# A state space by blocks of four tokens, and forty modulation chunks moved from one mixer to two feed-forwards

## The reference, cut to what matters

```python
# the state space: 16 groups g of 16 channels h, 64 complex states p each, tokens s
ab = exp((lr + 1j * li) * dt)                      # one complex factor per state (ab_re, ab_im)
bu[s, g, p] = sum_h ug[s, g, h] * bb[g, p, h]      # complex
x[s] = ab * x[s - 1] + bu[s]                       # the scan over the tokens
y[s, g, h] = Re(sum_p c[g, h, p] * x[s, g, p]) + d_skip[g, h] * ug[s, g, h]
z = gelu(y);  y_c = z * sigmoid(z @ w_glu + b_glu)
```

```python
mod   = silu(c)    @ w_mod[l] + b_mod[l]    # 6 * 1024 columns: sh1, sc1, g1, sh2, sc2, g2
mod_c = silu(c_cx) @ w_mod[l] + b_mod[l]
```

## Time and profile before

| | us |
|---|---|
| median of 3 runs | 1832.56 |
| lowest, highest | 1821.2, 1836.75 |
| the profiled execution | 1824.21 |
| its span, first to last instruction | 1822.4 |

### The profile page before, as it was taken

The page is one execution under the profiler, slowest core; times in us unless marked ns, Lnnn a source line. Parts: engine busy times, 40 slices in busy tenths (PEclk is TensorE's granted clock), DMA queues, the critical chain, the costliest instruction groups (busy, mean ns, idle before and its releaser), DMA issues.

```text
span 1822.4 us, 28979 instructions
## 1 busy us (share of the span) xinstructions
PE 1780.3 (98%) x9846; PEld 1443.9 (79%) x9846; DVE 804.6 (44%) x1556; ACT 903.1 (50%) x1410; POOL 1378.4 (76%) x811
## 2 busy tenths in 40 slices
PE   9989999999999999999999999999999999999997
PEld 7768888766888887788888977788888987788886
DVE  5566773674454554443112555441114665441112
ACT  6455443645544544555444455564436445554443
POOL 7359997546988878578888884578887894678884
PEclk9999999999999999999999999999999999999999
DMA  7767785687878646346665552346654563346551
GB/s 272 192 215 255 257 263 198 213 278 272 287 264 259 227 139 191 109 140 192 202 194 175 171 185 93 126 153 206 196 187 149 172 208 105 112 149 193 189 188 70
DMA packets 259110, 348.28 MB, mean 191 GB/s; under 512 B 20936, under 2 KB 161608, under 8 KB 259016
## 3 DMA queue, kind: packets, MB, share of 16 engines
q1 hardware_dynamic: 255840, 340.44, 58.1%
q10 hardware_dynamic: 3176, 6.62, 1.2%
HBM read 343.24 MB, written 1.64 MB: 189 GB/s over the span
## 4 chain that ended last, share of the span: by engine, by line
PE 89%; DVE 5%; ACT 2%; issue 1%; DMA 1%; POOL 1%; SPq 0%; ACTq 0%; DVEq 0%; POOLq 0%
PE bank L2402 23%; PE bank L2404 23%; PE bank L2403 23%; PE bank L2541 2%; PE bank L3119 2%; PE bank L2472 1%; PE bank L2470 1%; PE bank L2471 1%; PE bank L3109 1%; PE bank L3158 1%; PE bank L2507 1%; PE bank L2774 1%; PE bank L2565 0%; ACT wh L859 0%; DVE X L1552 0%
## 5 line engine op out<-in xcount | busy, mean ns | idle before, releaser
L827 POOL TENSOR_TENSOR wl<-raw,wh 128x1024 fp32r<-128x1024 f32 x300 | 734.4, 2460 | 101.7 <-ACT wh L1024 78.0
L2402 PE MATMUL bank<-wh,xh 128*128 128x512 f32 (+1 forms) x1590 | 625.2, 393 | 9.6 <-POOL wl L787 2.8
L2404 PE MATMUL bank<-wl,xh 128*128 128x512 f32 (+1 forms) x1590 | 611.4, 385 | 0.0
L2403 PE MATMUL bank<-wh,xl 128*128 128x512 f32 (+1 forms) x1590 | 610.0, 384 | 0.0
L786 POOL TENSOR_TENSOR wl<-raw,wh 128x512 fp32r<-128x512 f32 (+1 forms) x232 | 310.7, 1339 | 282.9 <-ACT wh L859 282.8
L1024 ACT ACTIVATE wh<-raw 128x1024 fp32r<-128x1024 f32 x270 | 286.7, 1062 | 430.2 <-PE bank L2404 417.6
L859 ACT ACTIVATE wh<-raw 128x1024 fp32r<-128x1024 f32 (+2 forms) x268 | 275.4, 1049 | 167.4 <-PE bank L2404 89.5
L2402 PEld LDWEIGHTS bank<-wh,xh 128*128 128x128 f32 x1590 | 299.0, 188 | 73.9 <-issue 8.5
L2404 PEld LDWEIGHTS bank<-wl,xh 128*128 128x128 f32 x1590 | 298.7, 188 | 60.9
L2403 PEld LDWEIGHTS bank<-wh,xl 128*128 128x128 f32 x1590 | 299.4, 188 | 54.8
L787 POOL TENSOR_TENSOR wl<-raw,wh 128x512 fp32r<-128x512 f32 (+1 forms) x232 | 310.5, 1339 | 0.0
(11 more groups left out here) (399 smaller groups left out, 2041.3 us busy)
## 6 DMA issues: line engine op xcount, KB each, us to landing
raw<-in_w_ffn_in SPq DMA_DIRECT2D x264, 256.0 KB, 2.9
raw<-in_w_in SPq DMA_DIRECT2D x224, 256.0 KB, 2.9
raw<-in_w_ffn_out SPq DMA_DIRECT2D x132, 256.0 KB, 2.9
raw<-in_w_mod SPq DMA_DIRECT2D x120, 256.0 KB, 4.4
raw<-in_l_w_gate SPq DMA_DIRECT2D x88, 256.0 KB, 3.7
raw<-in_l_w_up SPq DMA_DIRECT2D x88, 256.0 KB, 4.4
raw<-in_l_w_down SPq DMA_DIRECT2D x88, 256.0 KB, 4.2
arena<-in_w_mod SPq DMA_DIRECT2D x36, 512.0 KB, 5.5
```

What stands on the lines that cost most here:

```text
L827: nc.gpsimd.tensor_tensor(wl[:, s, :], raw[:, s, :], words(wh)[:, s, :], ALU.subtract)\
L2402: mm(dst, x_hi, w_hi, start=first, stop=False, skip_group_check=True)
L2403: mm(dst, x_lo, w_hi, start=False, stop=False, skip_group_check=True)
L2404: return mm(dst, x_hi, w_lo, start=False, stop=last, skip_group_check=True)
```

## The change

**Modulation.** Of layer 1 only tiles 0 and 1 (8 chunks) stay on PE in the second mixer. The other ten tiles go the second way: ten blocks in `ffn_c0` and ten in `ffn_x0`, the feed-forwards of the two streams in layer 0 of the second block. These get DVE's 16 operations a step, the loads beside the ring, and `mod_add` and `mod_turn` at their ends.

**State space.** The tokens are taken in blocks of four. A group of 16 channels is laid out so that 4 tokens by 32 channels of a pair fill the 128 partitions, and 64 blocks are the columns: `block_rows` does this with 64 fp32 matmuls of 32 columns on strips. `drive(c)` now serves four pairs at once (8 matmuls of 64 columns with full weights), so that there are two rounds c = 0, 1 and not eight. The scan runs over blocks with the fourth power of the decay, four pairs in one scan row, all on DVE; POOL has no part in it. `state(c)` adds, for each of the 4 tokens of a block, what the state of the block before gives (8 matmuls of 63 columns) and what the block's own tokens give (4 matmuls of 64 columns with the matrix `near`, d_skip in it); these are on strips of 32 columns. `near` comes from `near_products` (32 matmuls of 128 columns on strips, twice) and `near_matrix` on DVE. The tables `bpow`, `cpow` and the powers of the factor are made in `discretise` and `state_tables`. The 1 MB load of `c_re` and `c_im` in the mixer and ACT's negation of `c_im` go; smaller tables are loaded with `b_re` and `b_im`. ACT's Gelu reads the bank itself, and DVE's skip operations go.

```diff
-PE_MOD_TILES = (3, 12)
-LATE_MOD = {"ffn0": (0, 3, 8), "ffn1": (0, 7, 10)}
+PE_MOD_TILES = (3, 2)
+LATE_MOD = {"ffn0": (0, 3, 8), "ffn1": (0, 7, 10), "ffn_c0": (1, 2, 10), "ffn_x0": (1, 7, 10)}
+MOD_TURN = {"ffn0": 1, "ffn1": 3, "ffn_c0": 4, "ffn_x0": 5}
...
-    plan.modulation("mod1_lat", 1, w_mod[1], 3)
-    each = {n: (1, w_mod[1]) for n in range(3)}
-    plan.gemm("uq", a["l1_w_uq"], [384] * 3, modulated=each)
-    plan.gemm("ukv", a["l1_w_ukv"], [512] * 3, modulated=each)
-    plan.modulation("mod1_rope", 1, w_mod[1], 3)
-    for u in range(2 * MH):
-        plan.modulation(f"mod1_mla{u}", 1, w_mod[1], 2)
-    plan.gemm("out1", a["l1_w_out"], [512] * 2, pair=0, k_groups=[range(2, KD), range(0, 2)], modulated={0: each[0]})
+    plan.gemm("uq", a["l1_w_uq"], [384] * 3)
+    plan.gemm("ukv", a["l1_w_ukv"], [512] * 3)
+    plan.gemm("out1", a["l1_w_out"], [512] * 2, pair=0, k_groups=[range(2, KD), range(0, 2)])
     plan.modulation("mod1_norm", 1, w_mod[1], 4)
...
-                if name == "out1":
-                    for j in range(POOL_STATES, SSM_J):
-                        spin(j)
-                        state(j)
...
-                reduced(th16, ki, kf)
-                n = spread(C_("count").unsqueeze(1), SSM_J, 16)
-                step(v.tensor_tensor(angle[:, :, 0:16], n, spread(th.unsqueeze(2), SSM_J, 16), ALU.mult))
-                step(v.tensor_tensor(angle[:, :, 16:], n, spread(th16.unsqueeze(2), SSM_J, 16), ALU.mult))
+                step(v.tensor_scalar(th4, th, float(SSM_L), None, ALU.mult))
+                step(v.tensor_scalar(th64, th, 16.0 * SSM_L, None, ALU.mult))
+                settle()
+                reduced(th4, ki, kf)
+                reduced(th64, ki, kf)
...
-                step(v.tensor_tensor(cs, cos_n[:, :, 1], mag, ALU.mult))
-                step(v.tensor_tensor(sn, sin_n[:, :, 1], mag, ALU.mult))
-                settle()
-                step(v.tensor_scalar(cs, cs, -1.0, None, ALU.add))
+                step(v.tensor_copy(mag_pow[:, :, 0], mag))
+                step(v.tensor_tensor(mag_pow[:, :, 1], mag, mag, ALU.mult))
+                settle()
+                step(v.tensor_tensor(mag_pow[:, :, 2], mag_pow[:, :, 1], mag, ALU.mult))
+                step(v.tensor_tensor(mag_pow[:, :, 3], mag_pow[:, :, 1], mag_pow[:, :, 1], ALU.mult))
+                settle()
+                step(v.tensor_tensor(lam_re, cos_n[:, :, 21:21 + SSM_L], mag_pow, ALU.mult))
+                step(v.tensor_tensor(lam_im, sin_n[:, :, 21:21 + SSM_L], mag_pow, ALU.mult))
+                settle()
+                sn = lam_im[:, :, 0]
+                step(v.tensor_scalar(cs, lam_re[:, :, 0], -1.0, None, ALU.add))
+                for d in range(3):
+                    step(v.tensor_copy(back_re[:, :, d], lam_re[:, :, 2 - d]))
+                    step(v.tensor_copy(back_im[:, :, d], lam_im[:, :, 2 - d]))
                 settle()
...
+                n = SSM_L - 1
+                t0, t1 = (x[:, 0:n * SSM_J * SSM_G].rearrange("p (j s c) -> p j s c", j=SSM_J, s=n) for x in ptmp)
+                br, bi = (x[:, :, 0:n, :] for x in bpow)
+                step(v.tensor_tensor(br, powers(b0, n), factors(back_re, n), ALU.mult))
+                step(v.tensor_tensor(t0, powers(b1, n), factors(back_im, n), ALU.mult))
                 yield
-                settle()
-                v.tensor_tensor(bbar[0], bbar[0], btmp[0], ALU.subtract).then_inc(b_bar, 1)
-                v.tensor_tensor(bbar[1], bbar[1], btmp[1], ALU.add).then_inc(b_bar, 1)
+                step(v.tensor_tensor(bi, powers(b1, n), factors(back_re, n), ALU.mult))
+                step(v.tensor_tensor(t1, powers(b0, n), factors(back_im, n), ALU.mult))
...
+            def block_decay(c):
+
+                by_block = decay.rearrange("p (j b) -> p j b", j=4)
+                step(v.tensor_copy(by_block, spread(mag_pow[:, 4 * c:4 * c + 4, 3:4], 4, SSM_N)))
+                settle()
+                step(v.memset(by_block[:, :, 0:1], 0.0))
+
+            def near_matrix(c):
+
+                dve.wait_ge(near_mm, c + 1)
+                for jj in range(4):
+                    j = 4 * c + jj
+                    ins = v.scalar_tensor_tensor(out=near[:, j, :], in0=ident, scalar=V_("d_skip", j), in1=scratch[:, P * jj:P * jj + P],
+                                                 op0=ALU.mult, op1=ALU.add)
+                    ins.then_inc(near_set, 1) if jj == 3 else step(ins)
+
             undivided_norm("mix1", "l1_mix_pre", accb)
+            near_matrix(0)
+            block_decay(0)
...
             latent_rows(0)
+            near_matrix(1)
...
+                for c in range(SSM_T):
+                    dve.wait_ge(bu_done, c + 1)
+                    if c:
+                        block_decay(c)
+                    b, n = drive_bank[c], slice(SEQ * c, SEQ * c + SEQ)
...
-            for _ in range(5):
+            for _ in range(2):
                 next(ssm)
...
-            for _ in range(3):
-                next(ssm)
...
                 v.reciprocal(rinv[:, u % 4:u % 4 + 1], rsum[:, u % 4:u % 4 + 1]).then_inc(at_rinv, 1)
-                next(ssm, None)
                 if u + 2 < 2 * MH:
                     mla_top(u + 2)
+                next(ssm, None)
...
+                if f"ffn_{name}" in LATE_MOD:
+                    ffn(f"ffn_{name}", sg2, h2, mod_blocks(f"ffn_{name}"), ahead=ahead)
+                    rest_of_mod(f"ffn_{name}")
+                else:
+                    ffn(f"ffn_{name}", sg2, h2, ahead=ahead)
                 return lambda: gated_ffn(f"ffn_{name}", dst)
...
+            def near_products(c):
+                if c:
+                    pe.wait_ge(near_set, c)
+                for j in range(4 * c, 4 * c + 4):
+                    for i in range(2):
+                        for q in range(SSM_L):
+                            ins = mm(scratch[32 * q:32 * q + 32, P * (j % 4):P * (j % 4) + P], bpow[i][:, j, SSM_L - 1, :],
+                                     cpow[i][:, j, 3 - q:7 - q, :].rearrange("p d c -> p (d c)"), start=i == 0, stop=i == 1,
+                                     skip_group_check=True)
+                ins.then_inc(near_mm, 1)
+
+            modulate("mod1_in", slice(0, 2))
+            pe.wait_ge(b_bar, 2)
+            pe.wait_ge(c_pow, 2)
+            near_products(0)
+            rows_turn("mix1", (0, 1))
+            modulate("mod1_in", slice(2, None))
...
+            def block_rows():
+                for j in range(SSM_J):
+                    for t in range(TT):
+                        at = SSM_N * j + 32 * t
+                        for q in range(SSM_L):
+                            ins = mm(ut_bank[32 * q:32 * q + 32, at:at + 32], proj[:, t, SSM_G * j:SSM_G * j + SSM_G],
+                                     ident.rearrange("p (b s) -> p s b", s=SSM_L)[:, q, :], start=True, stop=True, skip_group_check=True)
+                ins.then_inc(ssm_ut, 1)
+
+            def drive(c):
+                for jj in range(4):
+                    for i in range(2):
+                        at = SEQ * i + SSM_N * jj
+                        ins = mm(drive_bank[c][:, at:at + SSM_N], bt[i][:, 4 * c + jj, :], uT1[:, c, SSM_N * jj:SSM_N * jj + SSM_N],
+                                 start=True, stop=True, skip_group_check=True)
                 ins.then_inc(bu_done, 1)
 
-            def state(j):
-                pe.wait_ge(x_state, j + 1 + max(0, j + 1 - POOL_STATES))
-                y = state_bank[:, SEQ * (j // 4):SEQ * (j // 4) + SEQ]
-                for i in range(2):
-                    ins = mm(y, cz[i][:, j, :], z_cos[:, SEQ * i:SEQ * i + SEQ], start=j == 0 and i == 0, stop=j % 4 == 3 and i == 1,
-                             skip_group_check=True)
+            def state(c):
+                pe.wait_ge(near_set, c + 1)
+                pe.wait_ge(x_state, c + 1)
+                for r in range(SSM_L):
+                    at = SEQ * c + SSM_N * r
+                    for jj in range(4):
+                        mm(state_bank[32 * jj:32 * jj + 32, at:at + SSM_N], near[:, 4 * c + jj, SSM_G * r:SSM_G * r + SSM_G],
+                           uT1[:, c, SSM_N * jj:SSM_N * jj + SSM_N], start=True, stop=False, skip_group_check=True)
+                    for i in range(2):
+                        for jj in range(4):
+                            z = SEQ * i + SSM_N * jj
+                            ins = mm(state_bank[32 * jj:32 * jj + 32, at + 1:at + SSM_N], cpow[i][:, 4 * c + jj, 4 + r, :],
+                                     z_cos[:, z:z + SSM_N - 1], start=False, stop=i == 1, skip_group_check=True)
                 ins.then_inc(y_state, 1)
...
-            pe.wait_ge(b_bar, 2)
-            for b in range(3):
+            near_products(1)
+            for b in range(2):
                 b_turn(b)
             tile_chunk("in1", 1, 0)
-            pe.wait_ge(b_ev, 2)
-            b_turn(3)
+            for b in range(2, 4):
+                pe.wait_ge(b_ev, 2 * b - 2)
```

(28 more changed lines are left out.)

222 lines of the change are left out of this document (100 added, 122 removed).

## The result

Twenty runs of the changed kernel have a median of 1840.47 us (1837.91 to 1860.62); the kernel before, run beside it, has 1828.38. The ratio is 1.0081, with a 95% interval of 1.0058 to 1.0104: slower, by a little under 1%, where I forecast 0.3% faster. The profiled execution took 1850.9 us, a span of 1849.1, which is 26.7 more than the one before. The twenty runs of the kernel before also fall into two groups, ten up to 1824.21 and ten from 1832.56 on, so lower group against lower group the change costs some 16 us.

What follows compares the result with a forecast made beforehand. PE, busy 98% of the span, was taken as the bound. Terms +4.0 - 14.1 - 2.6 + 6.4 + 0.7 = -5.6 us gave 1818.6 from the profiled 1824.21, carried over to 1832.56 - 5.6 = 1827; range 1812 to 1841.

Steps and rivals of the forecast that it cites:

- Part B: The attention: chunks, drives and states leave PE, then a chain over PE, ACT and DVE sets 30 us; -14.1 us.
- Part E: Discretise: ten small operations more before the first mixer's residual, +0.7 us (0 to +2.5); tables in ffn0 cost nothing.
- Part A: Second mixer up to the attention: new PE work against removed chunks and drives, plus ACT and rope delays; +4.0 us.
- the held rope: Ahead of the attention: DVE's rope slowed by POOL working on out1's chunks beside it; 1.2 us more, in Part A.
- The strips: New matmuls on strips of 32 columns, in the second mixer: 0.035 us a record, between 0.027 and 0.063.
- the rival of 62 ns: Strip matmuls in the second mixer: each takes about 62 ns however short, 12 us more, 1839; chance 0.03.
- The cover at X: Ahead of the attention: first near_products stands where PE waits 2.01 us for DVE's X, so 2.0 us is covered.
- ACT's share: Ahead of the attention: out1's ring copies queue on ACT before the uq and ukv bank copies; 1.5 of 5.2 us counted.
- first rival: Attention: without chunks PE has gaps and the clock falls to 1.2 GHz; +8.4 us, 1835, slower than before; chance 0.17.
- Part C: Out1: four single modulation chunks leave PE, where no one waits, 0.66 us each; -2.6 us.
- Part D: ffn_c0 and ffn_x0: each gets mod_add and mod_turn, +3.2 us, twice +6.4; DVE work and loads hidden.
- the rival of the starving loads: The two later feed-forwards: SP's block loads wait for DVE's sums; 1.3 us lost in each of 20 steps, 1853; chance 0.06.

Runs made afterwards that it cites:

- e2_hold: The changed kernel with POOL waiting for the end of DVE's rope ahead of out1's first low half; 1834.83 us, ratio to before 1.0057.
- e5_ssm: The new state space alone, with all forty modulation chunks back on PE in the second mixer; 1833.16 us, ratio to the kernel before 1.0044.
- e6_mod: The kernel before with only the move of the forty modulation chunks, old state space kept; 1827.57 us, ratio 1.0027.
- e8_paced: The changed kernel with three port waits taken out and three matmuls of ones in each attention unit; 1822.58 us, ratio to before 0.9990.
- e3_pace: The changed kernel with six matmuls of ones into an idle bank in each of the attention's twelve units; median of six runs 1853.00 us.
- e9_twenty: The changed kernel with three port waits taken out and twenty of the forty chunks kept on PE in the second mixer; 1816.02 us, ratio to before 0.9928.
- e10_pauses: As e9_twenty, with POOL also waiting for DVE ahead of the first product's 13th chunk and twice in in_x0; 1816.00 us, ratio to before 0.9925.

## Why the prediction was wrong, by its own steps

In short, three steps failed: in Part B the chain of the attention, priced at 3.4 us a pair of units and with the chunks counted as lying on the path (the saving was 7.5 and not 14.1); in Part E the tables in ffn0, put at nothing (9.5 us); and in Part A the held rope and the clock at the turns. That 1840.47 lies within 1812 to 1841 says nothing for the working: the forecast stood on 1832.56, a run of the upper group, and errors of opposite sign met in it.

**Part A** (+4.0, from -2 to +9) came to +6.8, in its range, but by luck: its terms were wrong both ways. The strips are cheaper than I took: 64 records of 128 columns took 1.9 us, 0.03 each, and 128 of 32 columns 2.05, 0.016 each, in the timeline of PE:

```profile
331.79 1.93 PE L2872 MATMUL bank<-arena 128*32 128x128 f32 x64
...
357.69 2.12 PE L2892 MATMUL bank<-con,arena 128*32 128x32 f32 x128
359.74 0.36 PE L2423 MATMUL bank<-wh,xh 128*128 128x192 f32 x1
```

So the rival of 62 ns is out, as the earlier trace rows said. (By the figure that the Trainium skill, TensorE: Matmul & The Clock Gate, the section on the gap of 56 ns, has for its slower decode path, the 128 would take an estimated 7.9 us; they took 2.05.) With 96 records of state(0) in 1.35 us, and the drives as I had them, the new PE work was 10.3 us and not 15.5. Waits and clock took the place of the 5.2. The cover at X was 1.6 us (the wait fell from 2.01 to 0.42). Mis-sized were ACT's share, 2.4 for 1.5, and above all the rope: I saw the order (out1's low halves ahead of it) and the lock, and priced seven or eight held operations at 1.2 us, though the earlier trace rows had the price of one, some 1 us more than its own length. Its cost to PE was 3.8 (the wait 4.86 for 1.09), and 5.3 were given back by e2_hold. A wait of 2.35 for the latent rows (0.86 before) I had not seen, and the turns at the lower clock, 2.8 us, I had left out, though my first rival named that place. Against my +4.0 these are -5.2 for the strips, +0.4 for the cover, +0.9, +2.6, +1.5 and +2.8: 7.0, where 6.8 was measured.

**Part B** (-14.1, from -19 to -8) came to -7.5, just outside. Its sum gives the new length as 30 us; it was 36.6. The first step that failed is that 12.0 us of chunks lay on the path: taking them away gave, with what the lower clock took back, 0.4 beside the new state space and -0.3 beside the old (e5_ssm, e6_mod), while the new state space, for which I counted 5.3 us of PE, gave 7.1. I set the old length to PE because it was busy 40.00 of 44.10 us; PE was full because chunks had been put where it would else have waited for the scan on POOL, whose 30.00 us stood in the same row. The second is the size of what came next, the chain, which carries 22 of the 30: I took 3.4 us a pair; values to values took 4.2 at full clock (419.20 to 423.38) and 6.1 at half (407.30 to 413.40). The pair that I added up has no DVE in it. In the trace, in every pair from 408.82 on, DVE splits the values (L1432, L1434) ahead of the next reciprocal, for which ACT's scaling waits; DVE's rows and then ACT's:

```profile
420.06 0.42 DVE L1432 CAST xh<-bank 128x256 fp32r<-128x256 f32 x1 [0.26 <-PE bank L3011]
420.52 0.42 DVE L1434 TENSOR_TENSOR xl<-bank,xh 128x256 fp32r<-128x256 f32 x1
```

```profile
421.05 0.40 ACT L1236 ACTIVATE arena<-arena,small 128x128 f32<-128x128 f32 x1 [0.65 <-DVE small L2095]
```

These two, 0.86 us in the chain that ended last, are about the difference between 3.4 and 4.2. No run moved the split behind the reciprocal, so what that would give is open.

**The first rival, the clock,** did come: 0.73 in the mean and 0.52 from 405 to 415, so nearly all of that at 1.2 GHz, behind a first stretch with PE busy 8.35 of 13.80 us. A pair cost 1.9 us more at the lower level, where I had 1.4. It is part of the loss, not the whole.

**Part C** (-2.6) came to -0.9, because out1 began at the lower clock (0.77 over its first 10.55 us). With the clock held up, in e8_paced and e3_pace, out1 up to the turn of X was 2.3 us shorter: the step was right but for that.

**Part D** (+6.4) came to 3.1 and 3.4, full to the last: ffn_c0 189.95 of 189.95 us at 239 GB/s, so the rival of the starving loads is out. The adding in ffn_c0, from 1029.21 to the turn at 1031.51, took 2.3.

**Part E.** The ten small operations cost 0.3 (for 0.7). The sentence behind them, "The tables in ffn0 cost nothing: PE is full and DVE has room", is the largest error, 9.5 us: 7.6 of waiting and the rest at a clock of 0.90 in the 17 us behind it. DVE's room was a mean over the step; the new order put six operations into the six us between one split and the next hidden layer, each at POOL's length. I had used the same mechanism for the rope and didn't ask where else it would stand.

**The sum.** Without the accident in c0 the span would be 1836.3, 13.9 more than before; I had -5.6. Of the 19.5 between them ffn0 is 9.5, B 6.6, A 2.8, C 1.7 and the turn at X 0.5, less 0.4 in E and 1.1 in ffn1, whose clock was at 1.00 for 0.99.

What stays open: how much of the 7.5 us in the attention each cause has at an equal clock, since no run took the chunks away with nothing in their place and the clock held; what decides whether a DVE operation gets in after one POOL operation or after a whole row, and why the start had no accident in 24 runs of e9_twenty and e10_pauses, 12 of them without a wait there.

## What to carry to other kernels

An engine that is full may have been filled on purpose: before work is taken off it, ask what the others' loops would take per unit without it, here 6.8 us a round of POOL and DVE, and read both halves of a double edit alone. DVE work on SBUF operands beside a running GpSimd costs one of GpSimd's for each of its own, however small, so count operations and not columns, and put them where GpSimd pauses. Work that hides in the waits of a latency chain also keeps the clock up; with the same three waits taken out, moving half of the chunks away gave 1816.0 us and moving all of them 1824.2 (on two chips; the spans of the traces are 1814.2 and 1822.7), of which 3.5 us are that one feed-forward less took blocks.
